# Four merge steps of the mixer run as quarters, one quarter behind each chunk of the gated linear branch

## The reference

```python
y_a = rg_lru(...)                    # a: linear recurrence
y_b = gated_delta_rule_chunked(...)  # b: chunks of 64
y_c = stick_breaking_attention(...)  # c
o_d = gla_chunked(...)               # d: gated linear branch, chunks of 16
...
def step(state, xs):                 # inside gla_chunked, 16 chunks
    q_i, kd_i, v_i, gl_i = xs
    o_i = q_i @ state
    state = state * gl_i[..., :, None] + jnp.swapaxes(kd_i, -1, -2) @ v_i
    return state, o_i
...
gates = jax.nn.sigmoid(merge_in.reshape(b, s, N_BRANCHES, D_MODEL))
for n, y_n in enumerate((y_a, y_b, y_c, y_d)):
    merged = merged + gates[:, :, n] * jnp.einsum("bsc,cd->bsd", y_n, w_branch[n])
return merged @ w_out
```

## Time and profile before

| | |
|---|---|
| median of 3 runs | 2160.98 us |
| the profiled execution's own time | 2157.44 us |
| its span, first to last instruction | 2155.7 us |
| PE busy | 2033.0 us, 94% |
| DVE busy | 1244.4 us, 58% |
| ACT busy | 950.1 us, 44% |
| mean granted clock of PE | 0.945 |
| DMA | 442.91 MB, mean 205 GB/s |

### The profile page before, as it was taken

The page is one execution under the profiler, slowest core; times in us unless marked ns, Lnnn a source line. Parts: engine busy times, 40 slices in busy tenths (PEclk is TensorE's granted clock), DMA queues, the critical chain, the costliest instruction groups (busy, mean ns, idle before and its releaser), DMA issues.

```text
span 2155.7 us, 30475 instructions
## 1 busy us (share of the span) xinstructions
PE 2033.0 (94%) x12343; PEld 1709.5 (79%) x12343; DVE 1244.4 (58%) x1738; ACT 950.1 (44%) x1351; POOL 64.8 (3%) x145
## 2 busy tenths in 40 slices
PE   8999999989889999997999977999999999879998
PEld 7878788877368888886999933699999999748998
DVE  3763443522388898896555555455565555545554
ACT  4664401111167777773333425333353344453333
POOL 6000000000000000000000000000000000000000
PEclk9999978969899999998999998899999999879999
DMA  9883521105789999994555697256646546313652
GB/s 309 314 287 99 197 77 59 59 1 202 286 323 345 332 331 355 359 347 143 189 186 176 208 375 296 99 196 190 195 161 195 189 160 218 117 40 110 214 183 98
DMA packets 207532, 442.91 MB, mean 205 GB/s; under 512 B 8140, under 2 KB 158764, under 8 KB 183872
## 3 DMA queue, kind: packets, MB, share of 16 engines
q1 hardware_dynamic: 201584, 424.70, 56.7%
q0 software_dynamic: 5840, 16.71, 2.3%
HBM read 440.19 MB, written 1.20 MB: 205 GB/s over the span
## 4 chain that ended last, share of the span: by engine, by line
PE 69%; DVE 5%; ACT 4%; DMA 2%; issue 1%; SPq 0%; ACTq 0%; DVEq 0%
PE P L708 68%; DMA ring<-in_ada_w 1%; ACT merged L1530 1%; DVE w_lo L2087 1%; DVE h L2040 1%; DVE xs L2040 1%; ACT pT L1530 0%; DVE xs L2033 0%; PE P L1243 0%; ACT big L1530 0%; ACT st L1530 0%; DMA ring<-in_w_up 0%; DVE w_lo L2496 0%; ACT h L1530 0%; DMA ring<-in_w_gate 0%
## 5 line engine op out<-in xcount | busy, mean ns | idle before, releaser
L708 PE MATMUL P<-x_parts,w_hi 128*128 128x256 f32 x2560 | 458.2, 281 | 2.1 <-DVE w_lo L2087 2.1
L708 PEld LDWEIGHTS P<-x_parts,w_hi 128*128 128x128 f32 x2560 | 399.1, 189 | 8.9 <-DVE w_lo L2087 2.8
L2087 DVE TENSOR_TENSOR w_lo<-ring,w_hi 128x1024 fp32r<-128x1024 f32 x302 | 351.5, 1220 | 80.8 <-ACT w_hi L1562 80.5
L708 PE MATMUL P<-w_hi,x_parts 128*128 128x256 f32 (+2 forms) x1504 | 373.3, 335 | 3.1 <-DVE w_lo L2496 3.1
L708 PE MATMUL P<-x_parts,w_lo 128*128 128x256 f32 x1280 | 361.2, 282 | 0.0
L1562 ACT ACTIVATE w_hi<-ring 128x1024 fp32r<-128x1024 f32 x302 | 297.4, 1050 | 53.5 <-DMA ring<-in_ffn_w_down 50.2
L2496 DVE TENSOR_TENSOR w_lo<-ring,w_hi 128x1024 fp32r<-128x1024 f32 x240 | 280.6, 1221 | 29.3 <-ACT w_hi L1777 26.6
L708 PEld LDWEIGHTS P<-w_hi,x_parts 128*128 128x128 f32 x1504 | 261.3, 194 | 31.7 <-issue 4.0
L1777 ACT ACTIVATE w_hi<-ring 128x1024 fp32r<-128x1024 f32 x240 | 240.6, 1052 | 84.7 <-DMA ring<-in_w_up 28.6
L708 PEld LDWEIGHTS P<-x_parts,w_lo 128*128 128x128 f32 x1280 | 241.7, 189 | 0.0
L708 PE MATMUL P<-w_lo,x_parts 128*128 128x256 f32 (+2 forms) x752 | 237.8, 337 | 0.0
(11 more groups left out here) (460 smaller groups left out, 2590.9 us busy)
## 6 DMA issues: line engine op xcount, KB each, us to landing
ring<-in_ada_w SPq DMA_DIRECT2D x72, 1024.0 KB, 9.0
ring<-in_ffn_w_gate SPq DMA_DIRECT2D x44, 1024.0 KB, 5.5
ring<-in_ffn_w_up SPq DMA_DIRECT2D x44, 1024.0 KB, 8.0
ring<-in_ffn_w_down SPq DMA_DIRECT2D x44, 1024.0 KB, 4.9
ring<-in_w_in SPq DMA_DIRECT2D x40, 1024.0 KB, 8.1
ring<-in_w_gate SPq DMA_DIRECT2D x40, 1024.0 KB, 5.0
ring<-in_w_up SPq DMA_DIRECT2D x40, 1024.0 KB, 5.1
ring<-in_w_down SPq DMA_DIRECT2D x40, 1024.0 KB, 5.0
```

What stands on the lines that cost most here:

```text
L708: return pe.matmul(o, l, r, start=start, stop=stop, **kw)
L2087: dve.tensor_tensor(w_lo[:, slot, c:c + half], ring[:, slot, c:c + half], w_hi[:, slot, c:c + half].bitcast(F32), ALU.subtract).then_inc(s ...
```

## The change

The merge steps 11 to 14 are each cut into four quarters of three matmuls: three gate matmuls, three more, the last two with the first branch matmul, and the last three branch matmuls. One quarter follows each of the 16 chunk steps on PE. `merge_rest` is the part of ACT and DVE, unchanged, behind every fourth quarter. So one merge step more than before stands among the chunks, and every later merge step moves up one place, up to step 22; from step 23 on the order is the old one. Where two merge steps stood between `d_end` and `b_rows` (14 and 15), two still stand, but they are 15 and 16. Behind `b_end`, only step 23 stands ahead of step 24, where 22 and 23 did. The number of matmuls and of transfers is the same, and so is the order of the transfers.

```diff
-STEPS += _weave([("d_chunk", c) for c in range(16)], _MERGE[11:14])
-STEPS += [("d_end",), _MERGE[14], _MERGE[15], ("b_rows",), ("b_decay",), _MERGE[16], _MERGE[17], ("b_kk",), _MERGE[18],
-          ("b_nat",), _MERGE[19]]
+for c in range(16):
+    STEPS += [("d_chunk", c), ("merge_part", 11 + c // 4, c % 4)]
+    if c % 4 == 3:
+        STEPS.append(("merge_rest", 11 + c // 4))
+STEPS += [("d_end",), _MERGE[15], _MERGE[16], ("b_rows",), ("b_decay",), _MERGE[17], _MERGE[18], ("b_kk",), _MERGE[19],
+          ("b_nat",), _MERGE[20]]
 STEPS += _weave([(s, lv, half) for lv in range(1, 6) for s in ("b_y", "b_xy") for half in range(2)]
                 + [("b_uw",)] + [(s, c) for c in range(4) for s in ("b_w", "b_o")] + [("b_end",)],
-                _MERGE[20:22])
-STEPS += _MERGE[22:25] + [("angles",)] + _MERGE[25:30] + [("sines",)] + _MERGE[30:32]
+                _MERGE[21:23])
+STEPS += _MERGE[23:25] + [("angles",)] + _MERGE[25:30] + [("sines",)] + _MERGE[30:32]
...
-            def p_merge(k):
+            def begin_merge(k):
...
+            def p_merge(k):
+                begin_merge(k)
+                merge_part(k, 0, DT + 4)
+
+            def merge_part(k, first, last):
+
+                n, d = BRANCH_ORDER[k // DT], k % DT
+                for c in range(first, min(last, DT)):
                     mm(P[:, k % 2, 0:S], held["g"][:, c, (d % 2) * 128:(d % 2) * 128 + 128], xT[:, c, :],
                            start=c == 0, stop=c == DT - 1)
-                for c in range(4):
+                for c in range(max(first - DT, 0), last - DT):
                     x = mm(P[:, k % 2, S:2 * S], held["w"][:, c, (d % 4) * 128:(d % 4) * 128 + 128], yT[n][:, c, :],
                            start=c == 0, stop=c == 3)
-                t.tell(x, "branch_psum")
+                if last == DT + 4:
+                    t.tell(x, "branch_psum")
+
+            def p_merge_part(k, j):
+                if j == 0:
+                    begin_merge(k)
+                merge_part(k, 3 * j, 3 * j + 3)
```

More of the change, by code:

```diff
@@ L190, in weight_loads @@
             out.append(projections.pop(0))
-        elif step == "merge":
+        elif step == "merge" or step == "merge_part" and which[1] == 0:
             b, d = BRANCH_ORDER[which[0] // DT], which[0] % DT
@@ L1044, in p_merge @@
                     pe.wait_ge(sem("merged"), k - 1)
-                for c in range(DT):
+            def p_merge(k):
[4 more added lines that the diff above has]
+                for c in range(first, min(last, DT)):
                     mm(P[:, k % 2, 0:S], held["g"][:, c, (d % 2) * 128:(d % 2) * 128 + 128], xT[:, c, :],
                            start=c == 0, stop=c == DT - 1)
-                for c in range(4):
+                for c in range(max(first - DT, 0), last - DT):
                     x = mm(P[:, k % 2, S:2 * S], held["w"][:, c, (d % 4) * 128:(d % 4) * 128 + 128], yT[n][:, c, :],
                            start=c == 0, stop=c == 3)
-                t.tell(x, "branch_psum")
+                if last == DT + 4:
[4 more added lines that the diff above has]
+                merge_part(k, 3 * j, 3 * j + 3)
             def p_ada(n, layer=0):
@@ L1083, in _ @@
                         "b_kk": p_b_kk, "b_nat": p_b_nat, "b_y": p_b_y, "b_xy": p_b_xy, "b_uw": p_b_uw, "b_w": p_b_w,
-                        "b_o": p_b_o, "b_end": p_b_end, "merge": p_merge, "ada": p_ada}
+                        "b_o": p_b_o, "b_end": p_b_end, "merge": p_merge, "merge_part": p_merge_part, "ada": p_ada}
             def first_mixer():
@@ L1743, in _ @@
                          "d_end": a_d_end, "b_decay": a_b_decay, "b_nat": a_b_nat, "b_y": a_b_y, "b_uw": a_b_uw,
-                         "b_end": a_b_end, "merge": a_merge, "ada": a_ada}
+                         "b_end": a_b_end, "merge": a_merge, "merge_rest": a_merge, "ada": a_ada}
             def table(fn):
@@ L2387, in _ @@
                          "b_kk": v_b_kk, "b_nat": v_b_nat, "b_y": v_b_y, "b_xy": v_b_xy, "b_uw": v_b_uw,
-                         "b_w": v_b_w, "b_o": v_b_o, "b_end": v_b_end, "merge": v_merge}
+                         "b_w": v_b_w, "b_o": v_b_o, "b_end": v_b_end, "merge": v_merge, "merge_rest": v_merge}
             def layer_affine(i, g, b, name=None):
```

## The result

The changed kernel takes 2147.15 us (median of 6 runs, 2137.12 to 2147.86), the kernel before 2157.29 beside it (6 runs, 2153.75 to 2161.89). The ratio is 0.9943, with a 95% interval of 0.9926 to 0.9961. That is 12.3 us faster by the ratio (8.4 to 16.0 by its interval) and 10.1 by the medians, where 12.0 were forecast; the forecast time was 2149.0. The profiled execution took 2147.61 us. The mean granted clock was 0.951 to 0.958 in the six executions of the changed kernel, and 0.942 to 0.948 in the fifteen of the kernel before that ran beside the first four experiments, so the higher clock is not that of one execution alone.

The account below looks back on a forecast made before the run. PE was taken as the bound, its price among the chunks set by the clock, not by waits. Gains of 9.1 + 3.5 less 0.6 made 12.0 us, so 2161.0 - 12.0 = 2149.0 us, range 2143 to 2160.

Parts of the forecast that it names:

- The bound: Among branch d's chunks PE is the bound, its price set by the clock: 44.2 us at half clock in three falls.
- The quarters: Among the chunks: 15 pairs at 2.10 us and 16 quarters at 1.30 + 0.19 us, 55.3 us at full clock.
- the third rival: Among the chunks: most of the 0.19 us per change of matmul kind isn't paid, 2147 us; inside the 70% full-clock case.
- DVE and ACT keep up: Among the chunks: each state is ready 1.9 us before PE reads it, so waits cost nothing.
- The clock stays full: Among the chunks: full clock, since the longest bare stretch is 2.10 us against 4.1 us ahead of a fall; 70%.
- The rule of the Trainium skill that was weighed: Among the chunks: falls need idle gaps, so eleven of sixteen chunks stay at half clock, 21 us slower, 2182.
- The end of branch d: From the last quarter to b_rows: sums at full clock, a 2.5 us wait before step 16, 9.1 us gained.
- A fall in the new wait: At the idle 2.5 us before step 16 the clock may fall for a while; 0.6 us loss counted.
- The end of branch b: Behind b_end: one merge step fewer before step 24, less a new 1.65 us wait for y1; 3.5 us gained.
- The sum: Whole kernel: 9.1 + 3.5 - 0.6 = 12.0 us gained, forecast 2149.0 us.
- Falls once and does not come back soon: Among the chunks: clock stays low, 3.0 us more per chunk with its quarter, 2165 to 2197; 13%.
- The other two rivals on the slow side: Among the chunks: a few at half clock, about 2156, or a stall in every quarter, 2157; 17%, 2153 to 2162.

Follow-up runs that it names:

- the first four experiments: Changed kernel with merge steps whole (1.0024), halves behind every second chunk (1.0050), three steps spread evenly (1.0058), or four bare chunks first (0.9959); ratios against the kernel before.
- the thin spread: Changed kernel with only merge steps 11 to 13 among the chunks, two or three matmuls behind each, old order after; against the kernel before, ratio 1.0058.
- the later waits: Changed kernel with the waits for y3 and y1 put behind a merge step's eight gate matmuls; against the kernel before, ratio 0.9921.

## Why the prediction was right

*The bound.* PE, by its clock and not by waits, among the chunks. Right: PE was busy without a gap before and after, and the stage went from 66.9 us with three merge steps to 55.0 with four.

*The quarters.* Sixteen of them at 3.6 us a chunk were forecast, 55.3 us from the first matmul to the last. It was 3.47 us a chunk, and 53.4 us (283.99 to 339.00 - 1.61 = 337.39). A chunk with its quarter was counted 0.12 us too dear: the quarter takes 290.04 - 288.56 = 1.48 us, as forecast (1.49), but the half chunk ahead of it only 0.91 us (288.56 - 287.65), where a half between bare chunks took 0.99 (290.54 - 289.55). So most of the 0.19 us for changing between the kinds of matmul isn't paid. That is the third rival, at the size it was given.

*DVE and ACT keep up.* Right: no wait on PE in the stage.

*The clock stays full.* Right in the result, and only partly in its reason. The prediction took the shortest bare stretch ahead of a fall, 4.1 us, against a pair of 2.1 us. With halves, a fall came after 3.2 us, and with whole steps after 3.3; with two matmuls a chunk, it came with bare stretches of 2.1 us. What the runs show is a row of cases: three dense matmuls behind each chunk hold the clock, two or three do not, six behind every second chunk do not, twelve behind every fourth or fifth do not. What property of the mixture decides stays open. That three were enough is therefore in part luck: the argument for it would have called halves at 4.2 us a close case and two matmuls a chunk safe. The rule of the Trainium skill that was weighed (TensorE: Matmul & The Clock Gate, section "The HAM clock gate"), that an idle window brings the slow clock, is not what these traces show: the falls among these chunks came with PE busy. In weighing it, the prediction put two thirds of the stage at half clock, 44.2 of 65.7 us; 39.7 of these 65.7 us were, so that case would have been ten chunks and some 2179 us, not eleven and 2182. It changes nothing in the forecast, and no chunk ran at half clock.

*The end of branch d.* Sums 1.61 us after the last quarter (1.67 forecast), 340.82 - 339.00 = 1.82 us long (1.73), idle 2.38 us before step 16 (2.5). From the first chunk to `b_rows` it was 80.7 us before and is 69.8: 10.9 us gained, where 9.1 stood in the sum.

*A fall in the new wait.* Counted with 0.6 us. None came there; one more than before came in the levels of the delta rule, and the part from `b_rows` to the sums of `b_end` took 115.3 us instead of 113.8, a loss of 1.5 us. Whether the change brings this one isn't shown: with four whole merge steps the levels had two such falls too, and with the thin spread and the later waits one.

*The end of branch b.* 3.5 us forecast; from those sums to step 24 it was 489.22 - 474.35 = 14.9 us and is 480.42 - 469.08 = 11.3: 3.5 us.

*The sum.* 10.9 - 1.5 + 3.5 = 12.9 us in the part that the change touches, against 12.0 forecast, 12.3 by the ratio and 10.1 by the medians. In this pair of traces nothing was given back later. Two errors of the sum work against each other: 1.8 us more were gained at branch d than counted, and 0.9 more lost to a fall.

*The rivals.* "Falls once and does not come back soon" is real, but belongs to a thinner mixture: seen for 75.1 us with two matmuls a chunk. Its reason, that a single quarter is too short to bring the clock back, is half right: with four bare chunks first the clock came back with the first quarter, in the spread of two or three a piece of the same size didn't bring it back. The other two rivals on the slow side did not occur.

## What to carry to other kernels

Where an engine's list has a stretch of small matmuls and PE is the bound, read the granted clock of that stretch before looking for idle time: it can cost more than all waits there, with PE busy in every row (here 39.7 us at half clock, and no wait among the chunks). Independent dense matmuls should then be dealt out behind each small group and not kept whole, and the size of the pieces has to be tried on both sides: dealt out too thinly, or in pieces too far apart, they cost more here than left whole. And put a wait in front of the first instruction that needs it, not at the head of the step.

## What was not expected of the hardware

The same 48 merge matmuls among the same chunks gave a stage of 55.0 us in pieces of three, 76.6 in pieces of six, and 74.7 in pieces of twelve: the middle size was the slowest, though by little (the intervals of the two ratios, 1.0050 and 1.0024, overlap). And taking a quarter of them out made the stage longer by 29.8 us (84.8 against 55.0), since the clock then was at 0.50 for 75.1 us without a return, in the slowest of five executions. A piece of three dense matmuls brought the clock back in one trace and not in another. In every one of these stretches PE was shown as busy nearly all the time.
